# One layer of a mixed-mixer block on one core: first norm with its squares added by halves and the factor and the scale in one operation, two projection tiles interleaved by chunk, and the output norms' squares added on VectorE

## The chip, the core and the metric

The kernel runs on one core of a Trainium2 chip, all in fp32. A core has five engines that run their own instruction streams and meet through semaphores: TensorE (PE, matrix products into eight banks of PSUM), VectorE (DVE), ScalarE (ACT), GpSimd (POOL) and SyncE (SP). In this kernel SyncE, ScalarE and GpSimd issue DMAs between HBM and the on-chip memory (SBUF, here one array called `arena`). Within an engine everything runs in the order of the program. The metric is the device time of one execution in microseconds; lower is better.

## The reference

One transformer layer over a prompt of 2048 tokens and 8 samples of 8 tokens (2112 tokens in all), D = 1024. What matters here is the first norm with its modulation, the projection behind it, and the norm of each mixer's output:

```python
mod = jax.nn.silu(c) @ p['mod_w'] + p['mod_b']
sh1, sc1, g1, sh2, sc2, g2 = jnp.split(mod, 6, axis=-1)
h = _rms(x, p['norm_mix']) * (1.0 + sc1) + sh1     # x * rsqrt(mean(x*x) + EPS) * norm_mix
z = h @ p['w_in']                                   # xa, ga, gb, gc, xb, uc, q, k, v
...                                                 # out_a: RG-LRU, out_b: short convolution,
...                                                 # out_c: S5 with a GLU, out_d: dilated attention
mix = jnp.concatenate([out_a, out_b, out_c, out_d], axis=-1).reshape(Bn, L, 4, 256)
mix = mix * lax.rsqrt(jnp.mean(mix * mix, axis=-1, keepdims=True) + EPS)
x = x + g1 * ((mix.reshape(Bn, L, D) * p['out_norm']) @ p['w_out'])
...                                                 # then a second norm and a mixture of 32 experts
```

## The kernel before

**Layout and stages.** The tokens lie along the free axis: `hT` holds x transposed, 8 blocks k of 128 features, each with 2112 columns. `CHUNKS` cuts the columns into four of 512 and one of 64 (the samples). The list `SCHEDULE` (L315) names all steps of the kernel in one order; `run` lets every engine walk through that list and do its own part of each step, so the order within an engine is the order of the list, and engines meet only through semaphores.

**The modulation.** `mod_w` comes in 12 slices of 2 MB, worked off in pairs. Pairs 0 and 1 of them (the shift and scale of the first norm) are multiplied in `norm1` on TensorE (L2043), taken over by VectorE (`mod_rows`), turned by TensorE and become `modT` (shift) and `sc1` (scale times the norm's gain) in `mod_cols`. The other four pairs are the steps `modp` 0 to 3: TensorE multiplies (L2062), VectorE adds the bias (L1429, semaphore `mod_row`), SyncE stores the rows. The weights of `modp` 0 and 1 are loaded early. Those of 2 and 3 are issued by SyncE in step `modp` 1 and 2, behind its wait for `mod_row` (L524 to L531): the weights of `modp` 2 go out only when VectorE has done `modp` 1. All four products use bank 7, so TensorE starts `modp` p only when `mod_row` has reached p.

**The first norm (`norm1`).** Per chunk: ScalarE squares 8 x 512 columns into `sqb` (`squares`, L984); VectorE adds the 8 blocks with one reduction (`sums`, L1438); TensorE multiplies by a matrix of ones, which adds over the partitions (L2071); ScalarE makes the factor from it by Ln and Exp (`rstd`, L991 and L993, alone for chunk 0, in pairs for 1, 2 and for 3, 4); VectorE multiplies all 8 blocks by the factor in one operation (`scaled`, L1445); and the scale and shift are put on by ScalarE for blocks 0 to 4 (`affine`, L1001) and by VectorE for blocks 5 to 7 (L1451). There is one `sqb`, so the squares of the next chunk wait for the sums of this one. The order of these calls is written out by hand for each engine.

**The projection (`z`).** 12 tiles i of 128 output features, each over 5 chunks c, as step ("z", i, c): 8 products of 128x512, two records each in the trace (L2098), into bank n % 2, with n counting the steps; ScalarE copies the bank into `zst` (`evacuate`, L1033 for tiles 0 and 1, L1035 for the others), and at chunk 4 issues the store of the tile. TensorE starts step n only when step n - 2 has been copied. The weights of a tile lie in `wz[i % 3]`. Now the list goes z tile 0, `modp` 0, `s5par`, z tile 1, `modp` 1, z tile 2, `modp` 2, `s5tab` 0, z tile 3, `s5prep` 0, `modp` 3 and so on; `s5par` is a chain of some 200 small operations on VectorE with two calls to ScalarE.

**The output norms.** For mixers C, A and B: `sqC` (and so on) squares both halves of the output on ScalarE (L1089), TensorE sums them with the matrix of ones, two products accumulated for each chunk, into a ring of four banks (`out`, L2188), ScalarE takes Ln of each and Exp of all (L1097, L1099), VectorE multiplies (L1662). They stand among the steps `qkv`, `qkn`, `qkt` of 17 token tiles (`tile(i)`: products L2199 and L2203, turns L2212) and the mixers' own steps (`A` and `As`: LRU, `B`: short convolution, L1528 to L1542).

Of the kernel before, what the change touches and what calls it, by code (L numbers as in the profile page):

```python
# [9 lines left out]
ALU = mybir.AluOpType  # L10
# [3 lines left out]
P = 128  # L14
# [79 lines left out]
def build(nc, A, O):  # L94
    with ExitStack() as ctx:
# [184 lines left out]
        ssum = take(2 * 512, w_at + 3072 + T + 1024).rearrange("p (n t) -> p n t", n=2)  # L280
# [31 lines left out]
        def tile(i):  # L312
            return ([("qkv", i)] if i < NT else []) + ([("qkn", i - 1)] if 1 <= i <= NT else []) + ([("qkt", i - 2)] if i >= 2 else [])

        SCHEDULE = [("mod",), ("norm1",), *zc(0), ("modp", 0), ("s5par",), *zc(1), ("modp", 1), *zc(2), ("modp", 2), ("s5tab", 0), *zc(3),  # L315
# [5 lines left out]
                    ("gluo",), ("sqC",), *tile(0), *tile(1), ("tab",), ("outC",), ("Ac", 0), *tile(2), ("outCn",), ("A", 0), ("Aw", 0), ("Ac", 1),  # L321
                    *tile(3), ("tabs", 0), ("Ap", 0), ("As", 0), *tile(4), *tile(5), ("A", 1), ("Aw", 1), *tile(6), ("tabs", 1), ("Ap", 1), ("As", 1), *tile(7),
                    ("sqA",), ("B", 0), *tile(8), ("outA",), ("outAn",), *tile(9), ("tabs", 2), ("B", 1), *tile(10), ("sqB",), *tile(11), ("outB",),
# [71 lines left out]
        def batch(b):  # L395
            return range(4 * b, min(4 * b + 4, NT))
        TILES = {"A": 10, "s5prep": 4, "s5a": 4, "s5b": 5, "s5c": 8, "outA": 5, "outB": 5, "outC": 5, "glu": 10, "qkt": 1, "tab": 7}
# [81 lines left out]
        def _(sp):  # L479
            def mod(step):  # L480
# [21 lines left out]
                part(2)  # L502
                part(3)
                part(4)
                first(1)
                first(2)
# [3 lines left out]
                for p in range(2):  # L510
                    sp.wait_ge(S("mod_mm"), p + 1)
                    mod_pair(p)

# [19 lines left out]
            def z(step, i, c):  # L533
                if c == 0 and 1 <= i <= 9:
                    sp.wait_ge(S("z_mm"), 5 * i)
# [420 lines left out]
        def _(act):  # L956
# [19 lines left out]
            def norm1(step):  # L976
# [19 lines left out]
                def affine(c):  # L996
# [3 lines left out]
                    for k in range(AFK):  # L1000
                        link(act.activation(hT[:, k, t0:t0 + w], hT[:, k, t0:t0 + w], ACT.Identity,  # L1001
                                            bias=modT[:, k, 0:1], scale=sc1[:, k, 0:1]))
# [15 lines left out]
                evacuate(0, 2)  # L1018

            def z(step, i, c):  # L1020
                if i or c >= 3:
                    evacuate(i, c)

            def evacuate(i, c):
# [4 lines left out]
                n = 5 * i + c  # L1029
# [277 lines left out]
        def _(dve):  # L1307
# [124 lines left out]
            def norm1(step):  # L1432
                def sums(c):
# [4 lines left out]
                    link(dve.tensor_reduce(ssum[:, c % 2, 0:w], sqb[:, :, 0:w].rearrange("p k t -> p t k"), AX.X, ALU.add))  # L1438
                    dve.sem_inc(S("norm1_ss"), 1)

                def scaled(c):
                    t0, w = CHUNKS[c]
                    dve.wait_ge(S("norm1_rstd"), c + 1)
                    x = hT[:, :, t0:t0 + w]
                    link(TT(x, x, rst1[:, t0:t0 + w].unsqueeze(1).broadcast_to([P, KT, w]), ALU.mult))  # L1445
                    dve.sem_inc(S("norm1_x"), 1)

                def affine(c):
# [1140 lines left out]
```

## Time and profile before

| | us |
|---|---|
| median of three runs (lowest, highest) | 2557.11 (2552.63, 2557.8) |
| profiled execution, time | 2561.29 |
| its span in the trace | 2559.6 |
| TensorE busy | 2271.1 (89% of the span) |
| VectorE busy | 895.5 (35%) |
| ScalarE busy | 595.6 (23%) |
| GpSimd busy | 286.8 (11%) |

A span is what lies between the first and the last instruction of the trace. The granted clock (PEclk) is the share of TensorE's full speed that the chip allowed in a stretch: 1.00 is its upper level, 0.50 the lower, and a number between the two is a stretch that has both. A releaser in a timeline is what ended the idle time before an instruction: "ACTq L1003" is the queue of ScalarE at line 1003, "DMA arena<-mod_w" a transfer. Neighbouring instructions of one line stand in the timeline as one row with their count. The stages, read from the timeline: the first norm with z tiles 0 to 2 until about 220 us, the other z tiles with the S5 mixer until 547, query, key and value tiles with the mixers A and B and the output norms until 815, then attention, the output projection with the router, and the experts.

### The profile page before, as it was taken

How to read it: one execution, taken by the hardware profiler on the slowest of the kernel's cores; microseconds unless marked ns; L12 is line 12 of the kernel's file. 1: busy time of each engine (PE TensorE's matmuls, PEld its weight loads, DVE VectorE, ACT ScalarE, POOL GpSimd, SP SyncE). 2: the span in 40 equal slices, each digit the busy share in tenths (PEclk: the TensorE clock that was granted, in tenths of full speed). 3: DMA queues.
4: the chain of work that ended last, by engine and by line, in shares of the span. 5: the costliest groups of instructions: out<-in, count | busy, mean ns of one | idle time of the engine just before them, and what ended most of it. 6: DMA issues, size and time to landing. Idle time of an engine off the chain costs nothing. (4 is left out here: it accounts for less than half of the span.)

```text
span 2559.6 us, 27934 instructions
## 1 busy us (share of the span) xinstructions
PE 2271.1 (89%) x7615; PEld 1129.0 (44%) x7616; DVE 895.5 (35%) x2161; ACT 595.6 (23%) x1054; POOL 286.8 (11%) x460
## 2 busy tenths in 40 slices
PE   4698999999895778899999939999999999999993
PEld 1243555444453435455555424444444444444441
DVE  4546553026552333455566541111111111111211
ACT  3410010235441223334333211111111111111111
POOL 0001020100001000000021121111111111111111
PEclk8899999999897776899899959999999999999997
DMA  9224131422447434122145244675559798687862
GB/s 377 89 109 122 50 66 51 159 98 94 136 162 200 164 145 158 63 79 79 61 137 207 97 166 141 227 249 182 185 181 340 252 339 325 217 306 271 311 205 58
DMA packets 106526, 438.92 MB, mean 171 GB/s; under 512 B 14956, under 2 KB 53580, under 8 KB 85884
## 3 DMA queue, kind: packets, MB, share of 16 engines
q1 hardware_dynamic: 76160, 309.46, 32.5%
q0 software_dynamic: 26160, 113.16, 16.2%
q10 hardware_dynamic: 4112, 15.14, 1.5%
q8 instruction: 48, 0.79, 0.1%
q14 instruction: 46, 0.37, 0.0%
HBM read 356.39 MB, written 83.10 MB: 172 GB/s over the span
## 5 line engine op out<-in xcount | busy, mean ns | idle before, releaser
L2411 PE MATMUL bank<-arena 128*128 128x512 f32 x1120 | 495.8, 599 | 14.5 <-issue 14.5
L2098 PE MATMUL bank<-arena 128*128 128x512 f32 (+1 forms) x960 | 360.1, 535 | 19.5 <-ACTq L1003 19.5
L2411 PEld LDWEIGHTS bank<-arena 128*128 128x128 f32 x1120 | 213.5, 191 | 292.8 <-issue 292.8
L2327 PE MATMUL bank<-arena 128*128 128x512 f32 (+1 forms) x544 | 273.0, 636 | 0.3 <-DMA arena<-mix_d 0.3
L2098 PEld LDWEIGHTS bank<-arena 128*128 128x128 f32 x960 | 168.8, 192 | 207.0 <-issue 185.8
L2439 PE MATMUL bank<-arena 128*128 128x512 f32 x560 | 250.4, 600 | 9.0 <-issue 9.0
L1988 DVE COPY arena<-bank 128x512 f32<-128x512 f32 x50 | 34.6, 693 | 553.4 <-PE bank L2426 553.4
L2439 PEld LDWEIGHTS bank<-arena 128*128 128x128 f32 x560 | 103.6, 190 | 133.0 <-issue 129.9
L2327 PEld LDWEIGHTS bank<-arena 128*128 128x128 f32 (+1 forms) x544 | 99.4, 199 | 91.0 <-issue 90.1
L2250 PE MATMUL bank<-arena 128*128 128x64 f32 x568 | 98.4, 308 | 38.0 <-ACTq L1160 22.5
L1998 DVE TENSOR_TENSOR arena<-bank,arena 128x512 f32<-128x512 f32 (+1 forms) x50 | 34.5, 691 | 254.9 <-PE bank L2439 208.4
L2199 PE MATMUL bank<-arena 128*128 128x512 f32 (+1 forms) x272 | 119.9, 593 | 0.0
L1149 ACT ACTIVATE arena<-arena 128x256 f32<-128x256 f32 (+3 forms) x128 | 68.3, 534 | 216.8 <-DVEq L1706 215.6
L1703 DVE CUSTOM_DVE_ANT_0 arena<-bank,arena 128x256 f32<-128x256 f32 (+3 forms) x128 | 58.3, 456 | 163.7 <-PE bank L2231 128.5
L916 POOL DMA_INDIRECT o_y<-arena x50 | 79.3, 1585 | 299.0 <-DVE arena L2000 202.9
L2250 PEld LDWEIGHTS bank<-arena 128*128 128x128 f32 x568 | 89.2, 226 | 53.3 <-ACTq L1160 34.5
L2415 PE MATMUL bank<-arena 128*64 128x512 f32 x224 | 99.2, 594 | 6.2 <-issue 5.4
L1248 ACT COPY arena<-bank 128x512 f32<-128x512 f32 x52 | 30.6, 588 | 304.9 <-PE bank L2377 304.9
L1035 ACT COPY arena<-bank 128x512 f32<-128x512 f32 (+1 forms) x50 | 25.7, 513 | 322.5 <-PE bank L2098 322.5
L2416 PE MATMUL bank<-arena 128*64 128x512 f32 x224 | 99.3, 595 | 0.0
L2231 PE MATMUL bank<-arena 64*128 64x256 f32 (+3 forms) x256 | 73.6, 658 | 9.2 <-SPq L439 9.2
L2239 PE MATMUL bank<-arena 128*128 128x128 f32 x284 | 65.6, 325 | 17.6 <-ACTq L1151 17.6
(461 smaller groups left out, 2608.9 us busy)
## 6 DMA issues: line engine op xcount, KB each, us to landing
arena<-wg SPq DMA_DIRECT2D x32, 2048.0 KB, 12.2
arena<-wu SPq DMA_DIRECT2D x32, 2048.0 KB, 16.9
arena<-wd SPq DMA_DIRECT2D x32, 2048.0 KB, 8.4
arena<-mod_w SPq DMA_DIRECT2D x12, 2048.0 KB, 13.0
z_d<-arena ACTq DMA_DIRECT2D x12, 1056.0 KB, 6.5
arena<-z_d POOLq DMA_DIRECT2D x10, 1056.0 KB, 8.2
arena<-kc POOLq DMA_DIRECT2D x8, 1280.0 KB, 8.4
arena<-vc POOLq DMA_DIRECT2D x8, 1280.0 KB, 8.0
```

The costliest lines, as they stand in the source:

```text
L916: pool.indirect_dma_start(out=O["y"], out_offset=bass.IndirectOffsetOnAxis(ap=sidx[:, s:s + 1], axis=0), in_=yb[:, s], in_offset=None, com ...
L1149: link(act.activation(ssb[:, u % 4, 0:w], ssb[:, u % 4, 0:w], ACT.Exp, bias=nmax[:, u % 4:u % 4 + 1], accum_out=ost[:, (u // 4) % 2, u % 4 ...
L2098: ins = mm(bank[n % 2][:, 0:w], wz[:, i % 3, k, :], hT[:, k, t0:t0 + w], start=(k == 0), stop=(k == KT - 1))
L2199: mm(bank[i % 3][0:r], hT[:, k, t0:t0 + r], wqkv[:, k, 0:512], start=(k == 0), stop=(k == KT - 1))
L2231: mm(bank[u % 2][:, 0:128 * len(vt)], qkT[rr, h // 2, q], qkT[rr, 2 + h // 2, k], start=True, stop=True).then_inc(S("att_s"), 1)
L2239: ins = pe.transpose(bank[2 + u % 2][:, c * P:(c + 1) * P], ssb[:, u % 4, c * P:(c + 1) * P], ident)
L2250: ins = mm(bank[4][:, 64 * h:64 * h + 64], pt[:, u % 4, c * P:(c + 1) * P], v[:, t, 64 * h:64 * h + 64], start=(c == 0), stop=(c == len(vt ...
L2327: ins = mm(bank[5 + q][0:r], l, wo[:, k, 512 * q:512 * q + 512], start=(k == 0), stop=(k == KT - 1))
L2411: ins = mm(bank[bk][:, :], xgT[:, s, k, :], m[w][:, k, :], start=(k == 0), stop=(k == KT - 1))
L2415: gate = mm(bank[2][HIGH, :], xgT[:, s, k, LOW], wg[w][:, k, :], start=(k == 0), stop=(k == KT - 1), tile_position=(0, HB))
L2416: rise = mm(bank[3][LOW, :], xgT[:, s, k, LOW], wu[w][:, k, :], start=(k == 0), stop=(k == KT - 1), tile_position=(0, 0))
L2439: ins = mm(bank[4 + h][:, :], hhT[:, k, :], wd[w][:, k, 512 * h:512 * h + 512], start=(k == 0), stop=(k == 3))
```

## The change

- `sums`: the reduction of 8 blocks becomes three additions, of 4 blocks to 4, 2 to 2, and 1 to 1. `ssum` moves from the staging of z tile 1 to the third buffer of `wz`.
- `scaled`, for the four chunks of 512: eight operations, one per block, that multiply by scale and factor at once. The second step then only adds the shift (`shifted` on VectorE, `affine` on ScalarE with a scale of 1.0). For the samples it stays as it was.
- `rstd` is called for each chunk alone, and the calls stand in another order on ScalarE and VectorE.
- z tiles 0 and 1 alternate by chunk: (0,0), (1,0), (0,1), (1,1), and so on, and both stand ahead of `modp` 0, `s5par` and `modp` 1. `ZN` gives the place of a z step, in the place of 5 i + c. The ones-products of the first norm stand behind z(0,0), z(1,0) and z(1,1).
- SyncE loads `wz[1]` ahead of x's chunks 3 and 4, and `wz[2]` only behind the last ones-product of the norm.
- Output norms: a new step `oaC`, `oaA`, `oaB` on VectorE adds the two squared halves, and TensorE does one product for a chunk in the place of two, waiting for `out_added`.

```diff
-        ssum = take(2 * 512, w_at + 3072 + T + 1024).rearrange("p (n t) -> p n t", n=2)
+        ssum = take(2 * 512, w_at + 2048).rearrange("p (n t) -> p n t", n=2)
...
-        SCHEDULE = [("mod",), ("norm1",), *zc(0), ("modp", 0), ("s5par",), *zc(1), ("modp", 1), *zc(2), ("modp", 2), ("s5tab", 0), *zc(3),
+        SCHEDULE = [("mod",), ("norm1",), *(("z", i, c) for c in range(5) for i in range(2)), ("modp", 0), ("s5par",), ("modp", 1), *zc(2), ("modp", 2), ("s5tab", 0), *zc(3),
...
-                    ("gluo",), ("sqC",), *tile(0), *tile(1), ("tab",), ("outC",), ("Ac", 0), *tile(2), ("outCn",), ("A", 0), ("Aw", 0), ("Ac", 1),
+                    ("gluo",), ("sqC",), *tile(0), ("oaC",), *tile(1), ("tab",), ("outC",), ("Ac", 0), *tile(2), ("outCn",), ("A", 0), ("Aw", 0), ("Ac", 1),
...
-                    ("sqA",), ("B", 0), *tile(8), ("outA",), ("outAn",), *tile(9), ("tabs", 2), ("B", 1), *tile(10), ("sqB",), *tile(11), ("outB",),
+                    ("sqA",), ("B", 0), ("oaA",), *tile(8), ("outA",), ("outAn",), *tile(9), ("tabs", 2), ("B", 1), *tile(10), ("sqB",), ("oaB",), *tile(11), ("outB",),
...
                 part(2)
+                first(1)
                 part(3)
                 part(4)
-                first(1)
-                first(2)
...
                 for p in range(2):
                     sp.wait_ge(S("mod_mm"), p + 1)
                     mod_pair(p)
+                sp.wait_ge(S("norm1_mm"), 5)
+                first(2)
...
                     for k in range(AFK):
                         link(act.activation(hT[:, k, t0:t0 + w], hT[:, k, t0:t0 + w], ACT.Identity,
-                                            bias=modT[:, k, 0:1], scale=sc1[:, k, 0:1]))
+                                            bias=modT[:, k, 0:1], scale=1.0))
                     act.sem_inc(S("h_ready"), 1)
                 squares(0)
                 rstd(0)
                 squares(1)
+                rstd(1)
+                squares(2)
                 affine(0)
-                squares(2)
-                rstd(1, 2)
+                rstd(2)
                 squares(3)
                 affine(1)
                 evacuate(0, 0)
+                rstd(3)
+                evacuate(1, 0)
                 squares(4)
-                rstd(3, 4)
                 affine(2)
                 evacuate(0, 1)
                 affine(3)
+                evacuate(1, 1)
+                rstd(4)
                 evacuate(0, 2)
+                evacuate(1, 2)
...
-                    link(dve.tensor_reduce(ssum[:, c % 2, 0:w], sqb[:, :, 0:w].rearrange("p k t -> p t k"), AX.X, ALU.add))
+                    for h in (4, 2):
+                        link(TT(sqb[:, 0:h, 0:w], sqb[:, 0:h, 0:w], sqb[:, h:2 * h, 0:w], ALU.add))
+                    link(TT(ssum[:, c % 2, 0:w], sqb[:, 0, 0:w], sqb[:, 1, 0:w], ALU.add))
...
+                        for k in range(KT):
+                            x = hT[:, k, t0:t0 + w]
+                            link(STT(x, x, sc1[:, k, 0:1], rst1[:, t0:t0 + w], ALU.mult, ALU.mult))
...
-                        link(TS(hT[:, k, t0:t0 + w], hT[:, k, t0:t0 + w], sc1[:, k, 0:1], modT[:, k, 0:1], ALU.mult, ALU.add))
+                        link(TS(hT[:, k, t0:t0 + w], hT[:, k, t0:t0 + w], modT[:, k, 0:1], None, ALU.add))
...
                 sums(0)
                 mod_rows(0)
-                scaled(0)
+                sums(1)
                 mod_rows(1)
                 mod_cols(0)
                 mod_cols(1)
-                sums(1)
-                affine(0)
+                scaled(0)
+                shifted(0)
                 sums(2)
                 scaled(1)
-                affine(1)
+                shifted(1)
                 sums(3)
+                scaled(2)
+                shifted(2)
                 sums(4)
-                scaled(2)
-                affine(2)
                 scaled(3)
-                affine(3)
+                shifted(3)
                 scaled(4)
...
+            def out_add(step):
+                dve.wait_ge(S("out_sq"), OUTN["sq" + step[0][2]])
+                a, b = (buf[q][:, 0:T] for q in SQRS[step[0][2]])
+                link(TT(a, a, b, ALU.add))
+                dve.sem_inc(S("out_added"), 1)
...
-                if i == 0 and c == 0:
-                    sums(2)
-                if i == 0 and c == 1:
-                    sums(3)
+                if c == 0:
+                    sums(2) if i == 0 else sums(3) if i == 1 else None
+                if (i, c) == (1, 1):
                     sums(4)
...
-                pe.wait_ge(S("out_sq"), OUTN[step[0]])
+                pe.wait_ge(S("out_added"), OUTN[step[0]])
...
-                    for j in range(2):
-                        ins = mm(mx(n)[:, 0:w], ones, buf[SQRS[step[0][3]][j]][:, t0:t0 + w], start=(j == 0), stop=(j == 1))
-                    ins.then_inc(S("mx_full"), 1)
+                    mm(mx(n)[:, 0:w], ones, buf[SQRS[step[0][3]][0]][:, t0:t0 + w], start=True, stop=True).then_inc(S("mx_full"), 1)
```

## Rows read from the trace of the kernel before

**Rows 1.** The page, busy time by engine.

```profile
PE 2271.1 (89%) x7615; PEld 1129.0 (44%) x7616; DVE 895.5 (35%) x2161; ACT 595.6 (23%) x1054; POOL 286.8 (11%) x460
```

**Rows 2.** Timeline of TensorE: start, length, line, operation, count [idle before, releaser].

```profile
15.53 9.50 PE L2043 MATMUL bank<-arena 128*9 128x512 f32 x32 [15.53 <-DMA arena<-mod_w]
...
55.38 8.43 PE L2098 MATMUL bank<-arena 128*128 128x512 f32 x16
...
77.71 9.22 PE L2098 MATMUL bank<-arena 128*128 128x512 f32 x16 [12.13 <-ACTq L1003]
...
95.36 17.53 PE L2098 MATMUL bank<-arena 128*128 128x512 f32 x48 [7.40 <-ACTq L1003]
...
119.80 29.46 PE L2098 MATMUL bank<-arena 128*128 128x512 f32 x80
...
185.57 7.06 PE L2062 MATMUL bank<-arena 128*9 128x512 f32 x32
```

**Rows 3.** Timeline of VectorE's bias steps (L1429), and of SyncE's queue.

```profile
119.99 1.40 DVE L1429 TENSOR_TENSOR arena<-bank,arena 9x512 f32<-9x512 f32 x2 [17.56 <-PE bank L2062]
...
164.29 1.40 DVE L1429 TENSOR_TENSOR arena<-bank,arena 9x512 f32<-9x512 f32 x2
192.75 1.41 DVE L1429 TENSOR_TENSOR arena<-bank,arena 9x512 f32<-9x512 f32 x2 [27.06 <-PE bank L2062]
...
167.20 0.82 SPq L521 DMA_DIRECT2D arena<-mod_w  x2
```

**Rows 4.** Landing of x's chunk 1 (issued 9.29) and of mod_w (issued 167.62).

```profile
DMA to landing us min/median/max: 27.2/27.2/27.2
...
DMA to landing us min/median/max: 12.3/12.3/12.3
```

**Rows 5.** Timeline of TensorE in the output norms, and VectorE's last step of B(0).

```profile
573.97 8.94 PE L2188 MATMUL bank<-arena 128*128 128x512 f32 x20 [0.54 <-ACTq L1143]
...
692.07 9.24 PE L2188 MATMUL bank<-arena 128*128 128x512 f32 x16
...
705.14 7.09 PE L2199 MATMUL bank<-arena 128*128 128x512 f32 x16
...
737.70 7.53 PE L2188 MATMUL bank<-arena 128*128 128x512 f32 x20
...
701.41 2.36 DVE L1542 TENSOR_TENSOR arena<-arena 128x2112 f32<-128x2112 f32 x1
```

**Rows 6.** TensorE's busy time and granted clock (PEclk) in 78 to 82 us.

```profile
78.00:82.00 4.00, 4.00 (x5) 0.51 0.00 0
```

**Rows 7.** Timeline of ScalarE in the first norm.

```profile
34.37 0.69 ACT L991 ACTIVATE arena<-bank,arena 128x512 f32<-128x512 f32 x1 [8.02 <-PE bank L2071]
35.07 1.28 ACT L993 ACT_TABLE_LOAD   x1
...
37.18 3.63 ACT L984 ACTIVATE arena<-arena 128x4096 f32<-128x4096 f32 x1 [0.18 <-ACT arena L993]
46.13 4.21 ACT L1001 ACTIVATE arena<-arena 128x512 f32<-128x512 f32 x5 [5.33 <-DVEq L1422]
...
77.73 1.11 ACT L1033 COPY arena<-bank 128x512 f32<-128x512 f32 x1
```

**Rows 8.** Timeline of VectorE in the first norm: reduction and product.

```profile
25.11 7.03 DVE L1438 TENSOR_REDUCE arena<-arena 128x512 f32<-128x4096 f32 x1 [24.98 <-ACTq L985]
...
37.08 4.43 DVE L1445 TENSOR_TENSOR arena<-arena 128x4096 f32<-128x4096 f32 x1 [3.31 <-ACTq L994]
```

**Rows 9.** VectorE's groups by form: count | busy us, mean ns | idle before.

```profile
L1491 DVE SCALAR_TENSOR_TENSOR arena<-arena 128x2048 f32<-128x2048 f32 x6 | 14.1, 2354 | 0.2
...
L1528 DVE TENSOR_TENSOR arena<-arena 128x2048 f32<-128x2048 f32 x2 | 4.6, 2292 | 0.1
...
L1553 DVE TENSOR_TENSOR arena<-arena 128x1024 f32<-128x1024 f32 x2 | 2.5, 1228 | 0.1
...
L1555 DVE TENSOR_TENSOR arena<-arena 128x512 f32<-128x512 f32 x2 | 1.4, 695 | 0.1
```

More of the change, by code:

```diff
@@ L396, in batch @@
             return range(4 * b, min(4 * b + 4, NT))
+        ZN = {s[1:]: n for n, s in enumerate(s for s in SCHEDULE if s[0] == "z")}
         TILES = {"A": 10, "s5prep": 4, "s5a": 4, "s5b": 5, "s5c": 8, "outA": 5, "outB": 5, "outC": 5, "glu": 10, "qkt": 1, "tab": 7}
@@ L534, in z @@
                 if c == 0 and 1 <= i <= 9:
-                    sp.wait_ge(S("z_mm"), 5 * i)
+                    sp.wait_ge(S("z_mm"), ZN[i - 1, 4] + 1)
                     sp.dma_start(wz[:, (i + 2) % 3], A["w_z"][i + 2]).then_inc(S(f"ld_wz{(i + 2) % 3}"), 16)
@@ L1017, in norm1 @@
                 affine(3)
+                evacuate(1, 1)
+                rstd(4)
                 evacuate(0, 2)
+                evacuate(1, 2)
             def z(step, i, c):
-                if i or c >= 3:
+                if i >= 2 or c >= 3:
                     evacuate(i, c)
@@ L1028, in evacuate @@
                     act.wait_ge(S(f"z_stored{i % 2}"), 16 * (i // 2))
-                n = 5 * i + c
+                n = ZN[i, c]
                 act.wait_ge(S("z_mm"), n + 1)
@@ L1443, in scaled, with shifted @@
                     dve.wait_ge(S("norm1_rstd"), c + 1)
-                    x = hT[:, :, t0:t0 + w]
-                    link(TT(x, x, rst1[:, t0:t0 + w].unsqueeze(1).broadcast_to([P, KT, w]), ALU.mult))
+                    if c == 4:
+                        x = hT[:, :, t0:t0 + w]
+                        link(TT(x, x, rst1[:, t0:t0 + w].unsqueeze(1).broadcast_to([P, KT, w]), ALU.mult))
+                    else:
+                        for k in range(KT):
+                            x = hT[:, k, t0:t0 + w]
+                            link(STT(x, x, sc1[:, k, 0:1], rst1[:, t0:t0 + w], ALU.mult, ALU.mult))
                     dve.sem_inc(S("norm1_x"), 1)
-                def affine(c):
+                def shifted(c):
                     t0, w = CHUNKS[c]
                     for k in range(AFK, KT):
-                        link(TS(hT[:, k, t0:t0 + w], hT[:, k, t0:t0 + w], sc1[:, k, 0:1], modT[:, k, 0:1], ALU.mult, ALU.add))
+                        link(TS(hT[:, k, t0:t0 + w], hT[:, k, t0:t0 + w], modT[:, k, 0:1], None, ALU.add))
                     dve.sem_inc(S("hd_ready"), 1)
@@ L2026, in _ @@
             run({"modp": modp, "s5par": s5par, "norm1": norm1, "Ac": conv, "Ap": lru, "As": scan, "B": sconv, "s5tab": s5tab,
-                 "s5prep": s5prep, "s5a": s5_in, "s5b": s5_turn, "gluy": gluy, "gluo": gluo, "outAn": out, "outBn": out, "outCn": out,
+                 "s5prep": s5prep, "s5a": s5_in, "s5b": s5_turn, "gluy": gluy, "gluo": gluo, "outAn": out, "outBn": out, "outCn": out, "oaA": out_add, "oaB": out_add, "oaC": out_add,
                  "qkv": qkv, "qkn": qkn, "bar": barrier(dve),
@@ L2085, in z @@
                 t0, w = CHUNKS[c]
-                n = 5 * i + c
+                n = ZN[i, c]
                 if c == 0:
```

## The prediction

> **What bounds the kernel now.** The time is 2557.1 us (median of three runs, 2552.6 to 2557.8); the profiled execution took 2561.3 us, of which the trace covers 2559.6. I sum changes against the profiled execution and add them to the median. First the page: TensorE is busy 89% of the span [rows 1]. So I looked only where the change works, at the gaps between TensorE's groups there. There are two stretches.
>
> The first norm, 0 to 193 us. TensorE does the first projection group of z tile 0 at 55.4 and waits until 77.7 for the second and until 95.4 for the third; from 95.36 on there is no gap until 222 [rows 2]. Idle or nearly so between the groups: 12.1 and 7.4 us. In the same stretch stands a chain that costs nothing today: the modulation product of pair 0 (7.05 us) stands between z tile 0 and tile 1 and ends at 119.8, VectorE adds its bias from 119.99, runs the S5 parameters without a pause, and does the bias of pair 1 from 164.29 to 165.69; only then does SyncE issue the weights of pair 2 at 167.2 and 167.6, and the second lands 12.3 us later, at 179.9 [rows 3, 4]. That is 60.1 us (all but 12.3 of it on VectorE and SyncE) from the end of product 0 to the weights of product 2. TensorE fills it with z tile 1 (29.46), product 1 (7.05) and z tile 2 (29.46), 66 us, and needs the weights at 185.57: a slack of 5.7 us [rows 2, 4].
>
> The output norms, 546 to 745 us: their sums are 20 matmul records each (two for one product) at 574.0, 692.1 and 737.7 [rows 5]; the row of A shows 16 of them.
>
> **Part 1: the interleave, and how late z now ends (E).** Per chunk of 512 tokens and tile a z group takes 6.86 us at the full clock (29.46 us for a tile, less 1.75 for its last 64 columns, over 4), and 9.2 when TensorE comes from 12 us of idleness: the group at 77.7 [rows 2], where the granted clock is 0.51 at first, its lower level of 1.2 GHz, against 2.4 [rows 6]. The change orders the engines anew, so I walk them through from durations of rows.
> Squares of a chunk take 3.63, Ln 0.69, a table load 1.28 before each Ln and each Exp, Exp with its wait 0.8 (a load ends at 36.35 and the squares behind the Exp start at 37.18), the five shifts 4.21, one evacuation 1.1, all on ScalarE [rows 7]. On VectorE the reduction took 7.03 [rows 8], once 7.18; by halves it is 2.29 + 1.23 + 0.69 with two gaps of 0.03 = 4.27 [rows 9]. The product with the factor was 4.43 [rows 8]; in its place stand 8 operations of 128x512 with a scalar and two tensors, a size that the trace lacks. At 2048 columns this form took 2.35 where two tensors alone took 2.29, and those took 0.69 at 512 [rows 9], so I take 0.71; bounds are 2.35 / 4 = 0.59 and 0.69 + 0.06 x 2 = 0.81. With gaps, 8 x 0.74 = 5.9; at the bounds chunk work moves by 1 us and hides behind ScalarE's squares and shifts. VectorE's three shifts cost as before.
> - Chunk 1 of x lands at 9.3 + 27.2 = 36.5 [rows 4]: faster sums of chunk 0 gain nothing before it. Squares(1) 36.5 to 40.2, sums(1) to 44.6, mod_rows and the columns to 48, the ones-matmul 47.0 to 49.0 (at the low clock, 2.07), its factor on ScalarE to 51.7, squares(2) to 55.5.
> - affine(0) now stands behind rstd(1) and squares(2), so it runs 55.7 to 59.9; z(0,0) starts at 60.0, 4.6 us later than now, and takes 9.2: to 69.2.
> - sums(2) stands behind z(0,0) on TensorE, and ScalarE's rstd(2) waits for it until 70.2. Factor to 72.8, squares(3) to 76.6, affine(1) to 81.0, evacuation (0,0) to 82.2. TensorE finishes z(1,0) at 77.0 and waits for that: z(0,1) 82.3 to about 90.3 (part of it at the low clock), z(1,1) to 97.2, sums(4) short.
> - rstd(3), evacuation (1,0), squares(4), affine(2), evacuation (0,1), affine(3), evacuation (1,1) follow without a pause on ScalarE, 82.2 to 101.7; (0,2) has its inputs at 92.6 and its bank at 93.9, so TensorE no longer waits: (0,2) 97.5, (1,2) 104.3, (0,3) 111.2, (1,3) 118.1, the two short ones, **E = 128.4**.
> Without product 0, z 0 and 1 ended at 149.2 - 7.05 = 142.2. So the filled waits do bring 13.8 us.
> A rule against this part: rstd is now called five times, ten table loads for six. In the trace a load is 1.28 us, and 0.83 us behind it both the Exp and its wait are over [rows 7]. The Trainium skill (ScalarE: Activation LUTs, What ACT_TABLE_LOAD costs) gives 1.28 and a drain of about 1.38 behind it, 2.66 for a switch. By the page the five loads between 70.2 and 104 would put 6.9 us more on ScalarE, of which TensorE, with two banks ahead, would feel some 2: about 2574. By that rule no Exp could end 0.83 us behind its load; the trace disagrees, so 1.28 stands.
>
> **Part 2: what the gain runs into.** In the new order z tile 1 stands ahead of product 0. Product 0 runs E to E + 7.05. The chain of 60.1 us behind it is the same instructions, so the weights of pair 2 land at E + 67.2 = 195.6. Between, TensorE has only product 1 (it waits 1.7 us for the bias of pair 0, since both use one bank) and z tile 2: done at E + 7.05 + 1.7 + 7.05 + 29.4 = E + 45.2 = 173.6. It then idles 22 us. After that idleness product 2 runs at the low clock: 9.5 us, as the same shape took at 15.5 after 15 us idle [rows 2]. End 205.1, where it was 185.57 + 7.06 = 192.6 [rows 2]: **+12.5 us**. VectorE waits for just this product (27.06 us idle at 192.75) before its S5 tables [rows 3], and TensorE's next wait is for those, so the shift goes on whole.
> At nothing: the second load of wz, moved ahead of two parts of x, delays them by 512 KB, and squares(3) needs its part only at 72.8; the third load, moved behind sums(4) and past two mod pairs on SyncE's queue, lands near 103 and is used at 144; the sums' new place only forces that move; loading w_z[3] earlier helps nobody. If the cover were gone, each would cost a landing of some 3 to 12 us.
>
> **Part 3: output norms.** Each loses 4.1 products of 0.86 us (6.86 / 8), 3.5 us at the full clock, and gains one add of 2112 columns on VectorE, 2.36 us as the product at 701.4 [rows 5].
> - C: the add fits into VectorE's idle time behind tile 0. The sums took 8.9 us, 1.9 over their 7.07 for the low clock; halved 5.4: **-3.5**. The stages after it hang on TensorE's next tile, so it is passed on.
> - A: VectorE comes to the add only behind B(0), which ends at 701.41 + 2.36 = 703.8 [rows 5]. Today TensorE does these 20 records from 692.07, inside that wait, and goes on to tile 9 at 705.14. Now it waits until 703.8 + 0.2 + 2.36 = 706.4 and does ten records cold, 3.6 + 2.3 = 5.9, and tile 9 starts at 712.3: **+7.1**. Behind TensorE's wait stand tile 9 and all after it.
> - B: squares end 737.6, add to 740.1, ten records with one wait for Ln, to 743.5 for 745.1: **-1.6**.
> Together +2.0 (bounds -3.5 - 1.6 = -5.1 and +5).
>
> Sum: 12.5 + 2.0 = 14.5; profiled 2561.3 + 14.5 = 2575.8; median **2571.6 us**.
>
> **Rivals.**
> 1. ScalarE keeps TensorE fed (no wait at 77 to 82, no cold group there). E = 60.0 + 9.2 + 7 x 6.86 + 3.5 + 2 = 122.7, 5.7 earlier: 2565.9. For it: the order of evacuations was made for two banks. Against: affine(1) and evacuation (0,0) need the factor that waits behind z(0,0).
> 2. Faster: the load of pair 2 isn't late. If it lands before E + 45.2, product 2 ends at E + 52.3 = 180.7, 11.9 earlier than now, and with +2.0 the time is 2547.2. It needs the 60.1 us chain to be 22 us shorter; from about 14 us shorter the sum is below nothing. Against: VectorE's S5 part shows no gap that could close, and nothing in it is changed.
> 3. The add for A is early or TensorE's wait there is hidden: A costs nothing, -5.1 for the norms, 12.5 - 5.1: 2564.5. Against: VectorE's order.
> 4. The halves don't do what they say: three dependent adds take the reduction's 7.2. Then z(0,0) and the second wait move 2.9 each, 2577.4. The rows of 128x2048 and 128x1024 speak against [rows 9].
> 5. ScalarE is slower than I walk: with 0.3 us more at each of its some 16 steps from 60 to 106 the groups from (0,2) on wait for their banks, E by up to 5 later, 2576.6.
>
> **How the numbers follow.** Forecast 0.55; rival 1 0.15; 2 0.06; 3 0.08; 4 0.05; 5 0.11. The predicted time is the forecast's. The range goes from rival 1 and 3 with run spread (2561) to rivals 4 and 5 (2578); outside lie rival 2 and the tails. About 0.2% (5.1 us) can be told from no change. Faster: rival 2, 0.06. Same: the low ends of 1 and 3, 0.10. Slower: the rest, 0.84.
>
> **What would show it.** Timeline of TensorE: first z group at 60, last of tile 1 done near 128, a gap of about 22 us between z tile 2 and product 2 with mod_w's landing at its end, product 2 about 9 us long and ending near 205. Chain of VectorE still 44 us between the two bias steps. Output norm A: TensorE idle from 691 until VectorE's add, tile 9 near 712 + 12.5 - 3.5 = 721. Wrong it would be if the weights land before z tile 2 ends, if E is under 116 (the front's gain then meets the stall's price), or if the adds are hidden.

## The result, and the profile after

The changed kernel takes **2569.8 us** (median of six runs, 2567.2 to 2571.9), the kernel before on the same chip 2557.4 (2552.6 to 2561.2). The ratio is 1.0049, with a 95% interval of 1.0035 to 1.0062: 12.3 us or half a per cent slower. The forecast was 2571.6 us, 14.5 us slower. The profiled execution took 2571.9 us (before: 2561.3), its span is 2570.1.

The page after, busy time by engine, against [rows 1]. TensorE does 30 matmul records less and is 16 us less busy, and the kernel is longer all the same.

```profile
PE 2254.9 (88%) x7585; PEld 1119.2 (44%) x7586; DVE 896.3 (35%) x2202; ACT 599.2 (23%) x1060; POOL 287.6 (11%) x460
```

TensorE's timeline of the first 205 us of the changed kernel, against [rows 2] (start, length, line, operation, count [idle before, releaser]):

```profile
59.19 9.80 PE L2118 MATMUL bank<-arena 128*128 128x512 f32 x16 [10.54 <-ACTq L1005]
...
80.79 1.23 PE L2091 MATMUL bank<-arena 128*128 128x512 f32 x2 [4.08 <-DVEq L1448]
81.81 15.54 PE L2118 MATMUL bank<-arena 128*128 128x512 f32 x32
...
97.35 31.20 PE L2118 MATMUL bank<-arena 128*128 128x512 f32 x96
128.49 7.06 PE L2082 MATMUL bank<-arena 128*9 128x512 f32 x32
137.28 7.05 PE L2082 MATMUL bank<-arena 128*9 128x512 f32 x32 [1.73 <-DVEq L1437]
144.26 29.47 PE L2118 MATMUL bank<-arena 128*128 128x512 f32 x80
195.59 9.79 PE L2082 MATMUL bank<-arena 128*9 128x512 f32 x32 [21.86 <-DMA arena<-mod_w]
```

The first z group starts at 59.2, the second chunk at 81.8, and both tiles are done at 128.5; without product 0 that was 142.2. So the interleave does fill the waits. Then look at the last row: TensorE stands for 21.86 us, released by the transfer of `mod_w`, and product 2 takes 9.79 us at the lower clock and ends at 205.4, where it ended at 192.6 [rows 2].

VectorE's bias steps and SyncE's issue of those weights, against [rows 3], and the landing of the two parts:

```profile
135.67 1.41 DVE L1436 TENSOR_TENSOR arena<-bank,arena 9x512 f32<-9x512 f32 x2 [25.34 <-PE bank L2082]
...
179.94 1.40 DVE L1436 TENSOR_TENSOR arena<-bank,arena 9x512 f32<-9x512 f32 x2
...
182.85 0.82 SPq L523 DMA_DIRECT2D arena<-mod_w  x2
...
DMA to landing us min/median/max: 7.7/10.0/12.3
```

From the bias of pair 0 to that of pair 1 VectorE takes 44.3 us as before, then 1.5 us on SyncE and 12.3 us for the second part, issued at 183.3: landed at 195.6. The chain did not get longer. It lost its cover: z tile 1 (29.46 us of TensorE's work) no longer runs beside it.

The output norms, TensorE, against [rows 5]; the row of VectorE is the add for A:

```profile
587.07 5.43 PE L2206 MATMUL bank<-arena 128*128 128x512 f32 x10 [0.26 <-ACTq L1150]
...
716.59 5.54 PE L2206 MATMUL bank<-arena 128*128 128x512 f32 x10 [14.39 <-DVEq L1675]
721.97 7.09 PE L2216 MATMUL bank<-arena 128*128 128x512 f32 x16
...
756.97 5.57 PE L2206 MATMUL bank<-arena 128*128 128x512 f32 x10 [2.51 <-DVEq L1675]
762.37 7.09 PE L2216 MATMUL bank<-arena 128*128 128x512 f32 x16
...
714.12 2.36 DVE L1674 TENSOR_TENSOR arena<-arena 128x2112 f32<-128x2112 f32 x1
```

For A, TensorE waits 14.39 us for VectorE's add, in the time in which it did the products before, and tile 9 starts at 721.97 for 705.14. That is 16.8 us later; 10.2 of them were there before the wait, as the last turn ahead of it starts at 701.09 for 690.88.

### The profile page after: what moved, and what is told of

It is laid out like the page before. It is cut to its first block and busy times, and to the rows that moved or that the text cites. A ratio compares the mean times of both kernels' runs of the same rounds, so it can differ in the third digit from the quotient of the medians.

```text
span 2570.1 us, 27923 instructions
## 1 busy us (share of the span) xinstructions
PE 2254.9 (88%) x7585; PEld 1119.2 (44%) x7586; DVE 896.3 (35%) x2202; ACT 599.2 (23%) x1060; POOL 287.6 (11%) x460
## 5 line engine op out<-in xcount | busy, mean ns | idle before, releaser
L2118 PE MATMUL bank<-arena 128*128 128x512 f32 (+1 forms) x960 | 359.1, 534 | 10.5 <-ACTq L1005 10.5
L2118 PEld LDWEIGHTS bank<-arena 128*128 128x128 f32 x960 | 168.5, 191 | 196.3 <-issue 195.6
L2432 PE MATMUL bank<-arena 128*64 128x512 f32 x224 | 102.6, 611 | 6.2 <-issue 5.3
L2433 PE MATMUL bank<-arena 128*64 128x512 f32 x224 | 102.7, 612 | 0.0
## 6 DMA issues: line engine op xcount, KB each, us to landing
arena<-wu SPq DMA_DIRECT2D x32, 2048.0 KB, 14.8
```

The lines of the kernel that those rows point to most:

```text
L2118: ins = mm(bank[n % 2][:, 0:w], wz[:, i % 3, k, :], hT[:, k, t0:t0 + w], start=(k == 0), stop=(k == KT - 1))
L2432: gate = mm(bank[2][HIGH, :], xgT[:, s, k, LOW], wg[w][:, k, :], start=(k == 0), stop=(k == KT - 1), tile_position=(0, HB))
L2433: rise = mm(bank[3][LOW, :], xgT[:, s, k, LOW], wu[w][:, k, :], start=(k == 0), stop=(k == KT - 1), tile_position=(0, 0))
```

## Where the time goes, stage by stage

These marks are worked out from TensorE's groups in each trace (starts, but for product 2): the end of product 2; the last product of the GLU, which is the last step ahead of the output norms; the last turn of the query and key tiles, ahead of the barrier; the first and last score product of attention; the first product of the experts. All in us. The labels belong to the experiments below: e1_front, e2_norms and e3_modp0 are 1 to 3, e5_load is 4, e4_c_only is 5, e6_sums2 is 6, the second rows of the two kernels are 7, and e9_half, e10_zero and e11_tiny are 8. e9_half leaves out a part of the squares, so what follows has other numbers and its last column isn't to be compared.

```
kernel          product 2  last GLU  last turn  first score  last score  experts   span
before            192.6     546.6     805.5       815.0       1290.1     1527.7   2559.6
before, again     190.7     545.2     809.0       818.5       1291.3     1528.9   2556.5
changed           205.4     560.0     822.8       832.6       1299.4     1538.8   2570.1
changed, again    205.5     559.7     826.0       835.7       1303.0     1540.7   2569.8
e1_front          204.2     558.2     819.9       829.4       1304.1     1542.1   2572.5
e2_norms          191.2     545.5     808.2       817.5       1284.9     1522.5   2552.9
e3_modp0          178.1     530.9     793.4       803.1       1266.9     1505.1   2533.2
e5_load           191.2     546.0     808.1       817.9       1285.2     1523.0   2551.4
e4_c_only         179.2     533.1     790.9       800.2       1272.4     1509.7   2537.5
e6_sums2          174.1     527.3     785.1       794.4       1266.4     1504.0   2536.1
e9_half           190.3     544.0     803.4       812.9       1284.0     1521.7   2527.7
e10_zero          191.5     545.2     818.8       827.7       1294.9     1533.1   2560.6
e11_tiny          192.3     547.0     810.8       820.2       1285.7     1523.4   2552.4
```

Read the differences between columns. From product 2 to the last GLU it is 352.8 to 354.8 in all thirteen: what product 2 loses or gains is passed on whole, within 2 us. The stage of the norms (last GLU to last turn) is 258.9 to 263.8 in the four traces with C, A and B as before (257.8 and 257.9 with C alone changed), and scatters by 5 us between two traces of the same kernel. Attention has two groups, which is the subject of the last experiments.

## Experiments

**1. The front alone.** The changed kernel with the three `oa` steps gone from the list and

```diff
-                pe.wait_ge(S("out_added"), OUTN[step[0]])
+                pe.wait_ge(S("out_sq"), OUTN[step[0]])
...
-                    mm(mx(n)[:, 0:w], ones, buf[SQRS[step[0][3]][0]][:, t0:t0 + w], start=True, stop=True).then_inc(S("mx_full"), 1)
+                    for j in range(2):
+                        ins = mm(mx(n)[:, 0:w], ones, buf[SQRS[step[0][3]][j]][:, t0:t0 + w], start=(j == 0), stop=(j == 1))
+                    ins.then_inc(S("mx_full"), 1)
```

> The change without its third part: first norm, interleave and loads as in the changed kernel, the output norms as before (two products for a chunk, no add). Theory 1 (the stall at the weights of pair 2 makes the front slower, and the shift goes on whole): product 2 ends at 205.4 for 192.6, and attention's first product starts 12.7 to 13.5 us later than before, at about 828; median 2557.4 + 13 = 2570. Rival 2 (the front is about neutral and the norms cost the 12 us): median within 3 us of 2557. Rival 3 (a part of any shift is given back behind the barrier, in attention): start of attention +13, median only +6 to +9.

Measured: 2573.9 us for 2554.5, ratio 1.0071 (1.0045 to 1.0097), so 11 to 25 us slower. Product 2 ends at 204.2 and the first score product starts at 829.4, as theory 1 says. Rival 2 falls: the front alone makes the kernel slower. The median is 19.4 us above that of before in its batch, 6 more than theory 1's 13, but the interval reaches that; rival 3 (6 to 9 us) falls. The interval also overlaps that of the whole change (9 to 16 us), so the medians don't tell whether the norms add to the loss.

**2. The norms alone.** The kernel before with the three steps and the single product.

> The kernel before with the third part alone: VectorE adds the squared halves of C, A and B, TensorE does one product for a chunk. Theory 1 (only C gains, A has to wait for the add behind B(0)): C -3.8, A +6.6, B +0.5 (as it lay between the two traces), so attention starts 3.3 us later than 815.0, median 2560.7. Rival 2 (the adds are hidden): -3.8, 0 and -3.5, median 2550. Rival 3 (give-back behind the barrier): start of attention +3.3 and the median at 2557.

Measured: 2555.7 for 2554.5, ratio 1.0008 (0.9993 to 1.0023). The first score product starts at 817.5, between the 815.0 and 818.5 of the two traces of before. The median is 1.2 us above that of before, with an interval of -1.8 to 5.9 us. Theory 1 said 3.3 and rival 3 nothing: both are inside, and this run doesn't part them. Rival 2 said -7.4 and is outside. So halving these products brings nothing that can be measured. The rows say why: TensorE has the same 14.39 us wait for A's add (at 702.22), and from the tile behind C's sums (tile 2) to tile 9 it takes 129.0 to 130.4 us in the five traces in which it waits for A's add and does ten records, and 121.7 to 123.5 in the seven in which it waits for no add.

**3. Product 0 earlier, nothing removed.**

```diff
-*(("z", i, c) for c in range(5) for i in range(2)), ("modp", 0), ("s5par",), ("modp", 1)
+*(("z", i, c) for c in range(2) for i in range(2)), ("modp", 0), ("z", 0, 2), ("s5par",), ("z", 1, 2), *(("z", i, c) for c in (3, 4) for i in range(2)), ("modp", 1)
...
                 evacuate(0, 2)
-                evacuate(1, 2)
...
-                if i >= 2 or c >= 3:
+                if i >= 2 or c >= 3 or (i, c) == (1, 2):
```

> The changed kernel, all instructions kept, but product 0 stands behind z(1,1) in place of behind z(1,4), and the S5 parameters start behind z(0,2) (ScalarE's evacuation of z(1,2) stands behind them). Theory 1 (a chain of 60 us from product 0 to the weights of product 2 with too little work on TensorE beside it): VectorE starts the bias of pair 0 at about 110, the weights of pair 2 land near 171, TensorE's idle time of 21.9 us before product 2 falls to under 2 and product 2 ends near 179.5 for 205.4; median 2569.8 - 25 = 2545. Rival 2 (the idle time has another cause, as the DMA itself or VectorE's speed): idle time stays over 15 us and the median stays within 8 of 2569.8.

Measured: 2543.7 for 2554.5, ratio 0.9959 (0.9945 to 0.9972). It is 10.8 us faster than the kernel before, where the changed kernel was 12.3 us slower: 23 us, or 26 by the medians of the two batches as they stand. It has all instructions of the changed kernel. Its trace is that of its fastest execution (2535.1 us), so the marks up to product 2 are the safer reading: 178.1 for 205.4. TensorE's timeline of this kernel, z tile 2, product 2 and z tile 3, and VectorE's bias of pair 0:

```profile
141.60 29.46 PE L2117 MATMUL bank<-arena 128*128 128x512 f32 x80
171.00 7.05 PE L2081 MATMUL bank<-arena 128*9 128x512 f32 x32
177.98 29.46 PE L2117 MATMUL bank<-arena 128*128 128x512 f32 x80
...
109.77 1.41 DVE L1435 TENSOR_TENSOR arena<-bank,arena 9x512 f32<-9x512 f32 x2 [0.22 <-DVE arena L1488]
```

The idle time before product 2 is gone, and with it the low clock: 7.05 us for 9.79. The stall comes from where product 0, and VectorE's chain behind it, stand in relation to TensorE's work; rival 2 falls.

**4. The weights of pair 2 earlier, the order as changed.** In SyncE's `modp`, for p = 1:

```diff
+                if p == 1:
+                    sp.wait_ge(S(f"st_mod{(p + 1) % 2}"), 32)
+                    sp.wait_ge(S("modp_mm"), p + 1)
+                    mod_pair(p + 1)
                 sp.wait_ge(S("mod_row"), p + 1)
...
-                if 1 <= p < 3:
+                if p == 2:
```

> The changed kernel, but SyncE issues the weights of pair 2 when product 1 is done (its buffers are free then) and not only behind the bias of pair 1. Theory 1: the weights land before z tile 2 ends; what is late next is the bias of pair 1 itself, since all four products use one bank: VectorE ends it 44 us behind that of pair 0, at about 181.4. Idle time before product 2 falls from 21.9 to about 7.7 us and product 2 ends near 190.5, -14 to -15; median 2555.5. Rival 2 (the bias isn't the next limit, the load was all): idle time under 1 us, median 2547. Rival 3 (the load waits on something else): no change, 2569.8.

Measured: 2553.0 for 2554.5, ratio 1.0000 (0.9982 to 1.0017). TensorE's row of product 2, and VectorE's bias of pair 1 right ahead of it:

```profile
181.64 9.56 PE L2086 MATMUL bank<-arena 128*9 128x512 f32 x32 [7.83 <-DVEq L1441]
...
180.03 1.40 DVE L1440 TENSOR_TENSOR arena<-bank,arena 9x512 f32<-9x512 f32 x2
```

The wait falls from 21.86 to 7.83 us and its releaser is now VectorE in place of the transfer: the next limit is the one that theory 1 named, the shared bank. So of the 22 us, 14 were SyncE's issue and the landing, and 8 are VectorE's 44 us of S5 parameters.

**5. A and B as before, C changed** (on top of experiment 3): `oaA` and `oaB` gone, `out` takes one product for C and two for A and B.

> As e3_modp0 (product 0 and the S5 parameters early), and of the output norms only C is changed: A and B are as in the kernel before. Theory 1 (A's add costs TensorE 6.6 us and B's 0.5): attention starts 7.1 us earlier than in e3_modp0 (803.1), at 796.0, and the median is 2543.7 - 7 = 2536.6. Rival 2 (A and B are free): same start and median as e3_modp0. Attention itself, from its first product to the first product of the experts: 712.7 us in before and e1_front, 702.0 to 706.2 in the four kernels with the changed norms. Theory a (it varies from one execution to the next, whatever the norms): anything between. Theory b (the two adds of A and B at the end of the stage shift what loads beside what): 712.7 here.

Measured: 2538.5 for 2554.0, ratio 0.9948 (0.9933 to 0.9963), 5.2 us under experiment 3 as read by the medians; the two intervals overlap (0.9945 to 0.9972 there), so the times alone don't settle it. The rows do for A: the 14.39 us wait is gone, and from tile 2 to tile 9 it takes 121.7 us for 129.4, 7.7 less (theory 1: 6.6). C's sums took 1.4 us more this time (6.70 for 5.35, with nothing changed there), and behind tile 9 B's part takes 41.6 us for 40.4, so no cost of B's add shows. Together the stage takes 257.8 us for 262.5: 4.7 of the 7.1 that theory 1 names. Product 2 ended 1.1 us later, so the first score product is at 800.2 for the 796.0 expected. Rival 2 falls for A and stands for B. From the first score product to the experts it took 709.5 us, which is neither the 712.7 of theory b nor the 702.0 to 706.2 of the kernels with all three adds.

**6. The ones-product of chunk 2 ahead of z(0,0)** (on top of experiment 5):

```diff
                 mod_turn(1)
                 sums(1)
+                sums(2)
...
-                if c == 0:
-                    sums(2) if i == 0 else sums(3) if i == 1 else None
+                if (i, c) == (1, 0):
+                    sums(3)
```

> As e4_c_only, and the ones-product of chunk 2 stands ahead of z(0,0) on TensorE. Theory 1 (ScalarE's 9.5 us wait for the factor of chunk 2 behind z(0,0) is what holds z(0,1)): z(0,0) starts 2 to 3 us later, z(0,1) 3 to 4 us earlier than at 81.8, tile 1 ends and product 2 ends 3 to 4 us earlier than in e4_c_only, unless the weights of pair 2 are late by then (their chain hangs on VectorE's norm steps): then 0 to 2. Median 2534 to 2537. Rival 2 (the late start of z(0,0) is what counts): 2 to 3 us later than e4_c_only.

Measured: 2535.2 for 2554.0, ratio 0.9924 (0.9893 to 0.9954). TensorE's timeline:

```profile
60.80 2.08 PE L2090 MATMUL bank<-arena 128*128 128x512 f32 x2 [11.85 <-DVEq L1447]
62.66 15.12 PE L2118 MATMUL bank<-arena 128*128 128x512 f32 x32
77.62 1.02 PE L2090 MATMUL bank<-arena 128*128 128x512 f32 x2
78.48 13.90 PE L2118 MATMUL bank<-arena 128*128 128x512 f32 x32
```

z(0,0) starts 3 us later, z(0,1) at 78.5 for 82.4 without a wait, and product 2 ends at 174.1 for 179.2, 5.1 us earlier, somewhat more than the 3 to 4 expected: without the wait the pair of groups from z(0,1) on also takes 13.90 us for 15.07. What held the second chunk was the factor that waited behind z(0,0). This is the kernel with the lowest median here, 0.8% under the kernel before and 1.2% under the changed one; that it is faster than experiment 5 (3.3 us by medians of 5 and 10 runs, overlapping intervals) rests on the rows.

**7. Second traces of both kernels.**

> The kernel before, unchanged, for a second trace. Theory a (attention's length varies from one execution to the next): from attention's first product to the experts' first it takes other than 712.7 us, by some us, while the part ahead of the barrier repeats within 1 us (first product of attention at 815). Theory b (the length belongs to the kernel): 712.7 within 1 us.

> The changed kernel, unchanged, for a second trace. Attention's first product at 832.6 within 1 us. Theory a: attention takes another length than 706.2 by some us. Theory b: 706.2 within 1 us; then the changed norms' kernels do have a shorter attention than the others, and 7 of the 17.6 us that are lost ahead of the barrier come back there.

The start of attention repeats only within 3.5 us (818.5 for 815.0, 835.7 for 832.6), so that part of both expectations falls. By the measure that they name, from the first score product to the experts, it took 710.4 us for 712.7 and 705.0 for 706.2: both are outside theory b's 1 us, though the two kernels stay apart. From first to last score product, the measure from here on, it is 472.8 for 475.1, and 467.3 for 466.8: the changed kernel's attention, none of whose instructions changed, is 5.5 to 8.3 us shorter. Over all traces it is 471.1 to 475.1 where VectorE has at most one `oa` step, and 463.8 to 467.4 where it has all three.

**8. What shortens attention?** First TensorE's 20 products fewer, without the adds: in the kernel before, A and B take only half of their squares.

```diff
-                    for j in range(2):
+                    js = (0, 1) if step[0] == "outC" else (0,)
+                    for j in js:
...
```

> The kernel before, but the output norms of A and B take only the first half of the squares: one product for a chunk, no add (the sum of the second half is left out, so what follows has other numbers, and the experts' part isn't compared). Question: attention, from its first to its last score product, took 472.8 to 475.1 us in three traces with A and B as before, 472.0 and 472.2 with C alone changed, and 463.8 to 467.4 in five with all changed. Theory s (it hangs on TensorE's stream, 20 products fewer ahead of it): 464 to 468 here. Theory v (it hangs on VectorE's two adds): 472 to 475. For the price of the norms: without the wait for an add A and B give 1 and 3.5 us, so attention starts 4 to 5 us earlier than the 815.0 and 818.5 of before.

Then the adds without a product fewer:

> The kernel before with VectorE's three adds, but TensorE still does two products for a chunk: one on the sum and one by a matrix of zeros, which adds nothing. TensorE's stream has as many products as before. Theory s: attention takes 472 to 475 us from first to last score product. Theory v: 464 to 468. Price of the norms without any product saved: C 0, A starts behind the add at 706.4 as a cold group of 9.4 us, so +10.6, B +4.5; attention starts 13 to 17 us later than in before.

Then three steps on VectorE at the same places that do next to nothing:

```diff
+                dve.wait_ge(S("out_sq"), OUTN["sq" + step[0][2]])
+                link(dve.memset(sm[:, 380:382], 0.0))
+                dve.sem_inc(S("out_added"), 1)
```

> The kernel before, with three steps on VectorE at the places of the adds that wait for the squares as these do, but only set two unused columns to zero (0.07 us each); TensorE does two products for a chunk as before. Question: attention, first to last score product, took 471.1 to 475.1 us where VectorE has no add for A and B and 463.8 to 467.4 where it has. Theory n (it hangs on the three more instructions in VectorE's stream): 464 to 468. Theory t (on the 2.4 us that each add takes, or what they move): 471 to 475. Price ahead of the barrier: B's step makes VectorE wait up to 4 us for the squares with nobody behind it in need, so attention starts within 1.5 us of the 815.0 to 818.5 of before.

Measured, from first to last score product: 471.1 with the products gone (0.9 us from theory v, 3.1 from theory s, inside neither), 467.2 with the adds and all products (theory v), 465.5 with the three tiny steps (theory n). So the shorter attention goes with three more instructions in VectorE's stream and not with the time of the adds or TensorE's products. These are one trace each.

The traces do show where most of it lies: in TensorE's granted clock, in two stretches of under 10 us near the end. The same two groups (turned scores times v, then output projection) first in the kernel before, where the clock is 0.53 from 1230 to 1236, then in the changed one, where it is 1.00 from 1242.7 to 1248.5:

```profile
1230.81 1.81 PE L2250 MATMUL bank<-arena 128*128 128x64 f32 x8
1232.41 3.55 PE L2327 MATMUL bank<-arena 128*128 128x512 f32 x4
...
1244.11 1.00 PE L2267 MATMUL bank<-arena 128*128 128x64 f32 x8
1244.95 1.94 PE L2344 MATMUL bank<-arena 128*128 128x512 f32 x4
```

The same 24 records take 6.7 to 7.0 us in all six long traces and 4.6 to 4.9 in all seven short ones. 40 us on, 25 records take 8.7 to 8.9 us in the six long ones and 6.4 in six of the seven (8.9 in e2_norms). That is 4.4 of the 5.5 to 8.3 us. In the kernel before TensorE had no idle time from 1223.9 until the clock fell at about 1229. Why the clock stays up in the kernels with three more steps, no trace shows, and no experiment varied the moment at which a kernel comes to these stretches.

The medians don't bear it out either: between experiments 3 and 5 they moved by -5.2 us, as the norms' stage did (-4.7), with nothing of the 8 us by which attention differs in their traces, and experiment 2's median is not under that of before. Whether attention is shorter in most executions stays open.

Ahead of the barrier e9 starts attention at 812.9, 2 to 6 us earlier than the two traces of before (4 to 5 expected), and e11 at 820.2, 1.7 us beyond the later one and so 0.2 outside what was expected. e10 starts it at 827.7, 9 to 13 us later (13 to 17 expected); counted from the last GLU it is 14.7 and 9.8 us more than the two traces of before, and the sum that was expected (10.6 + 4.5) fits the first of them.

## Why the prediction was right, point by point

**The walk through the first norm** (the walk is Part 1's step-by-step sum) holds almost to the microsecond at its marks: z(0,0) at 59.2 (forecast 60.0), z(0,1) at 81.8 (82.3), product 0 at 128.5 (128.4). ScalarE's wait for the factor of chunk 2 behind z(0,0) was forecast to end at 70.2; its timeline in the changed kernel:

```profile
69.89 0.69 ACT L993 ACTIVATE arena<-bank,arena 128x512 f32<-128x512 f32 x1 [9.46 <-PE bank L2091]
70.59 1.28 ACT L995 ACT_TABLE_LOAD   x1
71.89 0.63 ACT L995 ACTIVATE arena<-arena 128x512 f32<-128x512 f32 x1
```

Inside it several terms were off. The operation with scale and factor took 0.753 us at 512 columns and not 0.71, inside its bounds. The shift alone is cheaper than scale and shift, which the forecast took as equal: ScalarE's five took 3.75 us for 4.21. z(0,0) was released by ScalarE, so the second counts there and the first lay beside ScalarE's squares; z(0,0) then took 9.80 us for 9.2. A z group was put at 6.86 us, but the numbers named for it (29.46 less 1.75, over 4) give 6.93, as the rows do. And ScalarE did not go on without a pause from 82.2: it stood 4.40 us before affine(3), at 97.05, for VectorE's products; TensorE, two banks ahead, did not feel it. That the end of tile 1 came out within 0.1 us is partly luck. ScalarE's and VectorE's groups by form, first before, then after (count | busy us, mean ns | idle):

```profile
L1001 ACT ACTIVATE arena<-arena 128x512 f32<-128x512 f32 x20 | 16.3, 816 | 7.1 <-DVEq L1422 5.3 <-DVEq L1446 0.9 <-ACT arena L1033 0.2
```

```profile
L1003 ACT ACTIVATE arena<-arena 128x512 f32<-128x512 f32 x20 | 14.5, 723 | 5.5 <-DVEq L1460 4.6 <-ACT arena L986 0.4
```

```profile
L1459 DVE SCALAR_TENSOR_TENSOR arena<-arena 128x512 f32<-128x512 f32 x32 | 24.1, 753 | 2.0 <-DVE arena L1447 0.6 <-DVE arena L1428 0.2
...
L1465 DVE TENSOR_SCALAR arena<-arena 128x512 f32<-128x512 f32 x12 | 5.9, 489 | 0.9 <-DVE arena L1459 0.3
```

93 ns less on ScalarE for each, 59 on VectorE (548 before), where one operation fewer goes with the operand. The Trainium skill has this for ScalarE (ScalarE: Activation LUTs, What ACT_TABLE_LOAD costs): each operand of one value per partition adds about 93 ns over an immediate. The trace agrees to the nanosecond (816 - 723), and I had not used it.

**The table loads.** After each load the next operation starts 0.02 us later in the changed kernel too (70.59 + 1.28, Exp at 71.89, above), and the walk with 1.28 came out. The drain that the Trainium skill (ScalarE: Activation LUTs, What ACT_TABLE_LOAD costs) puts behind it isn't seen in these rows.

**The stall** (Part 2) is right in size, cause and sequel: forecast 22 us idle, product 2 from 195.6 for 9.5 us, end 205.1; measured 21.86, 195.59, 9.79, 205.4. Experiments 3 and 4 show the cause from both sides. Against before the shift is 12.8 us by the two first traces (forecast 12.5); before has 190.7 in its second, so it is 12.8 to 14.8. The front alone (experiment 1) cost 11 to 25 us.

**The norms** (Part 3). Forecast +2.0. By the two first traces the stage is 3.9 us longer (262.8 for 258.9), by the second ones 2.5. C: tile 2 moves by 592.34 - 582.74 = 9.6 where the last GLU moved by 13.4, so -3.8 (forecast -3.5; -2.5 by the second traces). A: tile 9 moves by 721.97 - 705.14 = 16.8 where the turn ahead of the wait had moved by 10.2, so +6.6 (forecast +7.1), and +6.6 again by the second traces. B: the tile behind its sums moves by 762.37 - 745.06 = 17.3, so +0.5 (forecast -1.6), but -2.1 by the second traces, because tile 9 itself took 2.6 us longer in the second one of before. So B's price isn't known to better than that. One step in it did fail: "ten records with one wait for Ln", which I let run at the full clock. TensorE had waited 2.51 us for the add, and the granted clock fell; the ten records took 5.57 us in four of the five traces with this wait. Windows of TensorE in the changed kernel (stretch, length, busy, granted clock, DMA share, GB/s):

```profile
756.00:758.00 2.00, 1.03 (x2) 0.88 0.16 59
758.00:760.00 2.00, 2.00 (x3) 0.50 0.41 131
760.00:762.00 2.00, 2.00 (x5) 0.77 0.19 66
```

In experiment 2 the same group after the same wait took 3.88 us, without the fall:

```profile
743.98 3.88 PE L2193 MATMUL bank<-arena 128*128 128x512 f32 x10 [2.50 <-DVEq L1661]
```

There B came out at -1.2 against the first trace of before.

**The sum.** 12.8 and 3.9 make 16.7, and 17.6 us are lost at the first score product (17.2 by the second traces), 3 more than forecast. The forecast's "goes on whole" holds as far as the barrier. Behind it the traces give 8.3 and 5.5 us back in attention, some 4.4 of them by the granted clock, which the prediction did not have; at the end of the span 10.5 and 13.3 are left. That the medians moved by 12.3 us with an interval of 8.9 to 15.9 (0.35% to 0.62%) lets both 14.5 and a small give-back stand. The mechanism of the front is right; how near the total came, 14.5 for 12.3, is luck in so far as two things that the sum lacks pull against each other.

**The rivals.** Rival 1 (TensorE fed without a wait) fell: it stood 4.1 us from 76.7, and a part of z(0,1) ran at the low clock (0.50 from 82 to 84). Rival 2 (the load not late) is what experiment 3 made true, and its price was right: 9.9 us under the kernel before, measured 10.8 (7 to 14). Rival 3 (A hidden) fell by the 14.39 us row. Rival 4 fell: the halves take 2.29 + 1.23 + 0.69 us as summed. Rival 5 fell: from 81.8 on TensorE has no idle time until product 0 is done.

## What to carry to other kernels

Before you move work ahead, write down every chain that runs beside it, and on whose queue its transfers are issued: the 29 us of z tile 1 that were moved ahead had been the cover of a 60 us chain (44 us on VectorE, issue, landing) that no idle time showed. A saving in products counts only if the engine was busy then: products done inside a wait are free, and the same sum waiting for a step behind that wait costs all of it. If an interleave comes out slower, first look for the row with the new releaser; here moving product 0 and the steps behind it ahead gave 23 us back with every instruction kept.

## What the runs showed of the hardware

- The granted clock after a short wait isn't repeatable: after 2.5 us idle the same ten records took 3.88 us in one trace and 5.57 in four, and tile 9's first group, behind 3.34 and 2.99 us idle and one short sum, took 7.09 and 9.64 in the two traces of before. This is 2.6 of the 4.9 us by which that stage scatters.
- It can also fall with no idle time just before: in the kernel before it was 0.50 from 1229 to 1232, after 5 us of matmuls without a gap, and stayed at 1.00 at the same records of the changed kernel. Two such stretches make 4.4 us of attention's difference.
- After 21.6 to 21.9 us idle a product of 7.05 us took 9.79 and 9.74 in two traces, 8.37 in a third.
- At 128x512 an ACTIVATE on ScalarE took 93 ns less when its scale became the constant 1.0 in the place of one value per partition. A TENSOR_SCALAR on VectorE took 59 ns less with one such operand and one operation fewer.
- Attention, with instructions unchanged, took 463.8 to 467.4 us in seven traces with three more small or large steps on VectorE ahead of the barrier and 471.1 to 475.1 in six with at most one; what the steps have to do with it is open.
